# The routing weights of one tile of tokens scattered to memory instead of built by one-hot products, and the row products of the sparse tokens spread anew

## What is computed

```python
q = (xt @ w_pq).reshape(PEER_BLOCK, PEER_HEADS, 2, PEER_HALF)
s = jnp.einsum('thpd,hpkd->thpk', q, sub_keys)
v1, i1 = lax.top_k(s[:, :, 0], PEER_TOPK)
v2, i2 = lax.top_k(s[:, :, 1], PEER_TOPK)
cand = (v1[..., :, None] + v2[..., None, :]).reshape(PEER_BLOCK, PEER_HEADS, -1)
cidx = (i1[..., :, None] * N_KEYS + i2[..., None, :]).reshape(PEER_BLOCK, PEER_HEADS, -1)
top, pos = lax.top_k(cand, PEER_TOPK)
eidx = jnp.take_along_axis(cidx, pos, axis=-1)
g = jax.nn.softmax(top.astype(jnp.float32), axis=-1).astype(xt.dtype)
ue = u_tab[eidx]
a = jax.nn.gelu(jnp.einsum('thkd,td->thk', ue, xt))
ve = v_tab[eidx]
return jnp.einsum('thk,thkd->td', g * a, ve)
```

## Time and profile before

| | |
|---|---|
| median of 3 runs | 3568.3 us (3566.43 to 3577.35) |
| profiled execution: its time, its span | 3572.08 us, 3570.3 us |
| mean granted TensorE clock | 0.986 |
| PE busy | 3475.4 us, 97% of the span |
| DVE busy | 2467.0 us, 69% |
| ACT busy | 1462.7 us, 41% |
| mean rate of the DMA engines | 255 GB/s |

### The profile page before, as it was taken

One profiled execution on the slowest core, in us unless ns is written; L12 is line 12 of the kernel. 1 busy time (PEld: TensorE's weight loads), 2 busy tenths in 40 slices (PEclk: granted clock), 3 DMA queues, 4 the chain that ended last, 5 costly groups with the idle time before them and its releaser, 6 DMA issues.

```text
span 3570.3 us, 54219 instructions
## 1 busy us (share of the span) xinstructions
PE 3475.4 (97%) x18428; PEld 2973.7 (83%) x18428; DVE 2467.0 (69%) x4643; ACT 1462.7 (41%) x2544; POOL 895.4 (25%) x1026
## 2 busy tenths in 40 slices
PE   6999999999999999999999999999999999999998
PEld 5776889999999787777777777999999998777776
DVE  6455678889888775555464556888898878555554
ACT  3324233335877333333233333333367753333332
POOL 0010100003333534444400010000053345344442
PEclk9999999999999999999999999999999999999999
DMA  6354434447999998999744433444499999799995
GB/s 244 126 185 135 142 132 147 149 149 282 354 338 346 391 343 336 363 358 359 292 151 155 161 130 123 149 154 147 147 349 345 344 361 388 278 366 356 364 356 199
DMA packets 269536, 909.83 MB, mean 255 GB/s; under 512 B 32213, under 2 KB 65029, under 8 KB 268453
## 3 DMA queue, kind: packets, MB, share of 16 engines
q0 software_dynamic: 126352, 471.34, 35.9%
q1 hardware_dynamic: 106128, 385.92, 30.8%
q10 hardware_dynamic: 36868, 50.35, 3.8%
HBM read 792.14 MB, written 115.34 MB: 254 GB/s over the span
## 4 chain that ended last, share of the span: by engine, by line
PE 92%; DMA 3%; DVE 2%; issue 1%; POOL 1%; ACT 1%; SPq 0%; DVEq 0%; ACTq 0%; POOLq 0%
PE ps L441 15%; PE ps L443 15%; PE ps L442 15%; PE ps L1001 10%; PE ps L1003 9%; PE ps L1002 9%; PE ps L981 5%; PE ps L1015 3%; PE ps L810 2%; DMA urow<-in_u_rows,idu 1%; PE ps L866 1%; PE ps L937 1%; PE ps L485 1%; DMA hin<-expert_spill 1%; PE ps L887 1%
## 5 line engine op out<-in xcount | busy, mean ns | idle before, releaser
L441 PE MATMUL ps<-mov,whl 128*128 128x384 f32 (+1 forms) x2816 | 1008.8, 358 | 2.2 <-DVE whl L428 2.2
L443 PE MATMUL ps<-mov,whl 128*128 128x384 f32 (+1 forms) x2816 | 985.5, 350 | 0.0
L442 PE MATMUL ps<-mov,whl 128*128 128x384 f32 (+1 forms) x2816 | 984.2, 350 | 0.0
L428 DVE TENSOR_TENSOR whl<-raw,whl 128x1024 fp32r<-128x1024 f32 x648 | 792.5, 1223 | 206.8 <-ACT whl L418 202.5
L418 ACT CAST whl<-raw 128x1024 fp32r<-128x1024 f32 x648 | 679.5, 1049 | 87.4 <-ACT hst L1196 78.8
L1001 PE MATMUL ps<-whl,wgthl 128*128 128x512 f32 x1536 | 608.4, 396 | 19.6 <-DVE wgthl L1710 19.6
L700 POOL DMA_INDIRECT urow<-in_u_rows,idu x256 | 310.8, 1214 | 1208.8 <-DVE idu L1643 778.1
L1003 PE MATMUL ps<-whl,wgthl 128*128 128x512 f32 x1536 | 604.6, 394 | 0.0
L1002 PE MATMUL ps<-whl,wgthl 128*128 128x512 f32 x1536 | 603.4, 393 | 0.0
L441 PEld LDWEIGHTS ps<-mov,whl 128*128 128x128 f32 x2816 | 529.3, 188 | 40.1 <-issue 8.7
L442 PEld LDWEIGHTS ps<-mov,whl 128*128 128x128 f32 x2816 | 529.5, 188 | 30.5 <-issue 2.4
(11 more groups left out here) (261 smaller groups left out, 3623.0 us busy)
## 6 DMA issues: line engine op xcount, KB each, us to landing
raw<-in_uT_tab SPq DMA_DIRECT2D x256, 512.0 KB, 4.5
raw<-in_v_tab SPq DMA_DIRECT2D x256, 512.0 KB, 6.9
expert_spill<-hst ACTq DMA_DIRECT2D x256, 192.0 KB
hin<-expert_spill POOLq DMA_DIRECT2D x256, 192.0 KB, 7.9
gt<-weight_spill POOLq DMA_DIRECT2D x64, 768.0 KB, 8.8
weight_spill<-stage POOLq DMA_DIRECT2D x22, 2048.0 KB, 14.7
raw<-in_w_in SPq DMA_DIRECT2D x72, 512.0 KB, 4.7
raw<-in_w_mod SPq DMA_DIRECT2D x64, 512.0 KB, 3.6
```

The lines of the kernel that those rows point to most:

```text
L428: nc.vector.tensor_tensor(whl[:, m % RING, 1], raw[:, raw_n(m) % RAW], whl[:, m % RING, 0].bitcast(F32), ALU.subtract).then_inc(lo_done, 1)
L441: nc.tensor.matmul(o, w[:, 0, k], src[:, 0, k, :cols], start=(k == 0), stop=False)
L442: nc.tensor.matmul(o, w[:, 0, k], src[:, 1, k, :cols], start=False, stop=False)
L443: mm = nc.tensor.matmul(o, w[:, 1, k], src[:, 0, k, :cols], start=False, stop=(k == KC - 1))
```

## The change

The dense tokens are divided again. Two tiles (256 tokens, `OH`) keep the one-hot groups, 32 of them. The weights of the third tile (`N_TS = 1`) are no longer computed by PE: its part of `weight_spill` is filled with zeros at the start of each layer, four writes of 2 MB from a tile of zeros, and in each head the 16 weights of its 128 tokens are added there by 16 indirect DMAs of 128 single numbers each (`scatter_one`). DVE works out the places (`chosen`), and the softmax is made head by head (`shares`, with the exponential on ACT at slot 9 of each head).

The panels that stood beside the 16 groups move into the heads (`T_U = 10`, 12 panels for a head). The row products start in the second head: six beside each head but the first (42), then 12 in the first rest, 40 beside the 32 groups, 4 in the second rest, and 30 ahead of panel 23 of the second table. At the start of layer 0 the first two panels are split four and three chunks earlier.

```diff
-N_G = SD // GT
+N_TS = 1
+OHB = DB - N_TS
+OH = OHB * P
+N_OH = OH // TB
+N_G = OH // GT
-T_U = 8
+T_U = 10
-DOTS_V = 24
-DOTS = [0, 0] + [2] * (REST - 2) + [1, 2] * (N_G // 2) + [2] * (REST - 2) + [0, 0] + [1, 1, 2] * (DOTS_V // 3)
+DOTS_H = (0, 0, 0, 0, 0, 0, 0, 0, 0, 2, 2, 2)
+DOTS_A = sum(DOTS_H) * (PH - 1)
+DOTS_V = 23
+DOTS = ([0, 0] + [2] * (REST - 2) + [1, 1, 1, 2] * (N_G // 4) + [1] * 4 + [0] * (REST - 4)
+        + [1, 1, 2] * 7 + [1, 1])
...
+            for b in range(N_OH, NTB):
+                pool.dma_start(g_d[:, :, b].rearrange("a p x -> p a x"),
+                               zero[:].unsqueeze(1).to_broadcast([P, P // AG, P])).then_inc(zero_out, 16)
...
+            def scatter_one(h, n):
+
+                k, t = h * TOPK + n // N_TS, n % N_TS
+                settle(pool)
+                pool.indirect_dma_start(g_d.rearrange("a p b (x o) -> (a p b x) o", o=1),
+                                        bass.IndirectOffsetOnAxis(idg[:, t, k:k + 1], 0),
+                                        topv[:, OHB + t].rearrange("p h k -> p (h k)")[:, k:k + 1], None,
+                                        compute_op=ALU.add).then_inc(sc_out, 16)
+
+            def scatter(h):
+
+                pool.wait_ge(idg_ready, l * PH + h + 1)
+                pool.wait_ge(g_norm, l * PH + h + 1)
+                pool.wait_ge(sc_out, l * (16 * N_TS * SLOTS) + 16 * N_TS * TOPK * h)
+                for n in range(N_TS * TOPK if h + 1 < PH else 0):
+                    scatter_one(h, n)
...
+            for h in range(PH):
+                pool.wait_ge(idu_ready, l * PH + h + 1)
+                if h == 0:
+                    for k in range(UR):
+                        gather_u(k)
+                scatter(h)
+                if h + 1 < PH:
+                    for k in range(h * sum(DOTS_H), (h + 1) * sum(DOTS_H)):
+                        gather_u(k + UR)
...
                     if k + UR < SLOTS:
                         gather_u(k + UR)
+                    if left:
+                        scatter_one(PH - 1, left.pop(0))
...
                 if r == 1:
...
+                    pool.wait_ge(sc_out, (l + 1) * (16 * N_TS * SLOTS))
                     load_g(0)
                     load_g(1)
...
-                if not (l or which) and c >= KC - 3 and c < KC - 1:
-                    split_hi(act, l, c - (KC - 3))
+                if not (l or which) and c in (1, 3):
+                    split_hi(act, l, c // 2)
...
+                    if j == 9:
+                        act.wait_ge(g_sub, l * PH + h + 1)
+                        nc.scalar.activation(topv[:, :, h], topv[:, :, h], ACT.Exp).then_inc(g_exp, 1)
...
-                if not (l or which) and c >= KC - 1:
-                    split_lo(dve, l, c - (KC - 1))
+                if not (l or which) and c in (3, 5):
+                    split_lo(dve, l, c // 2 - 1)
...
+            def chosen(h):
+
+                hs = slice(h * TOPK, (h + 1) * TOPK)
+                first, second = sel1[:, OHB:DB, h], sel2[:, OHB:DB, h]
+                nc.vector.scalar_tensor_tensor(idf[:, 0, hs], sel1[:, DB, h], float(NKEYS), sel2[:, DB, h], ALU.mult, ALU.add)
+                nc.vector.scalar_tensor_tensor(place[:, 1], second, float(NTB * AG), first, ALU.mult, ALU.add)
+                chain.link(nc.vector.tensor_scalar(place[:, 0], first, -1.5, 0.25, ALU.add, ALU.mult))
...
                 for j in range(2 + T_U):
                     split_lo(dve, l, M_T + h * (2 + T_U) + j + LEAD)
                     if j < 2 and h:
                         key_of(h - 1, j)
+                    if j == 1 and h:
+                        chosen(h - 1)
+                    if j == 10:
+                        shares(h)
+                    if h:
+                        at = (h - 1) * sum(DOTS_H)
+                        dots_between(at + sum(DOTS_H[:j]), at + sum(DOTS_H[:j + 1]))
```

More of the change, by code:

```diff
@@ L164, in dots_by @@
 def dots_by(p):
-    return sum(DOTS[:p + 1])
+    return DOTS_A + sum(DOTS[:p + 1])
 assert dots_by(LATE_U + DOTS_V - 1) == SLOTS
@@ L295, in build_trunk @@
     dinv = sb("dinv", [P, TT * PH])
-    sel1T = sb("sel1T", [P, S])
-    sel2T = sb("sel2T", [P, S])
-    gT = sb("gT", [P, SD])
+    sel1T = sb("sel1T", [P, OH + P])
+    sel2T = sb("sel2T", [P, OH + P])
+    gT = sb("gT", [P, OH])
+    place = sb("place", [P, 3, N_TS, TOPK])
+    idg = sb("idg", [P, N_TS, SLOTS], U32)
     idf = sb("idf", [P, 2, P])
@@ L640, in _ @@
         pool.wait_ge(consts_made, 2)
+        for q in range(P // TB):
+            nc.gpsimd.iota(tokat[q * TB:(q + 1) * TB], [[P * AG, N_TS]], base=(N_OH + q) * AG * TB, channel_multiplier=1,
+                           allow_small_or_imprecise_dtypes=True).then_inc(tokat_made, 1)
         for half in range(2):
@@ L919, in _, with turn_rows @@
             spread_root(pe, 2, l * 4 + 4, l * 2 + 2)
+            def turn_rows():
+                for c in range(KC):
+                    o = ps[:, 4 + c // 4, c % 4 * P:(c % 4 + 1) * P]
+                    nc.tensor.matmul(o, mov[:, 0, c, SD:], identr[:], start=True, stop=False)
+                    mm = nc.tensor.matmul(o, mov[:, 1, c, SD:], identr[:], start=False, stop=True)
+                mm.then_inc(htok_turned, 1)
             def two_heads(two, first=False):
@@ L952, in experts @@
                         gemm(pe, l, first_m + j, more=i * 4, more_half=i * 2, cols=SD)
-            for c in range(KC):
-                o = ps[:, 4 + c // 4, c % 4 * P:(c % 4 + 1) * P]
-                nc.tensor.matmul(o, mov[:, 0, c, SD:], identr[:], start=True, stop=False)
-                mm = nc.tensor.matmul(o, mov[:, 1, c, SD:], identr[:], start=False, stop=True)
-            mm.then_inc(htok_turned, 1)
             for n in range(REST):
@@ L971, in _ @@
             settle(pe)
-            with pe.Fori(0, NTB // 2) as b:
+            with pe.Fori(0, N_OH // 2) as b:
                 for half in range(2):
@@ L1610, in key_of, with shares @@
                 chain.link(nc.vector.tensor_reduce((sel1, sel2)[side][:, :, h], eq[:], AX, ALU.add))
+            def shares(h):
+                dve.wait_ge(g_exp, l * PH + h + 1)
+                sums, share = den[:, h * TT:(h + 1) * TT], topv[:, :, h]
+                chain.link(nc.vector.tensor_reduce(sums, share, AX, ALU.add))
+                chain.link(nc.vector.reciprocal(dinv[:, h * TT:(h + 1) * TT], sums))
+                nc.vector.tensor_tensor(share, share, dinv[:, h * TT:(h + 1) * TT].unsqueeze(2).to_broadcast([P, TT, TOPK]),
+                                        ALU.mult).then_inc(g_norm, 1)
@@ new lines, in chosen @@
+            def chosen(h):
[4 more added lines that the diff above has]
+                chain.link(nc.vector.tensor_scalar(place[:, 0], first, -1.5, 0.25, ALU.add, ALU.mult))
+                nc.vector.tensor_scalar(idu[:, hs], idf[:, 0, hs], lbase[:], None, ALU.add).then_inc(idu_ready, 1)
+                chain.link(nc.vector.tensor_scalar(place[:, 0], place[:, 0], MAGIC, MAGIC, ALU.add, ALU.subtract))
+                chain.link(nc.vector.scalar_tensor_tensor(place[:, 2], place[:, 0], float(P * NTB * AG - AG), place[:, 1],
+                                                          ALU.mult, ALU.add))
+                if l == 0 and h == 0:
+                    dve.wait_ge(tokat_made, P // TB)
+                for t in range(N_TS):
+                    last = nc.vector.tensor_scalar(idg[:, t, hs], place[:, 2, t], float(TB), tokat[:, t:t + 1],
+                                                   ALU.mult, ALU.add)
+                last.then_inc(idg_ready, 1)
@@ L1612, in _, with dots_between @@
+            def dots_between(k0, k1):
+                for k in range(k0, k1):
+                    if k == 0:
+                        dve.wait_ge(htok_ready, l + 1)
+                    dve.wait_ge(u_in[k % UR], l * 16 * len(range(k % UR, SLOTS, UR)) + 16 * (k // UR + 1))
+                    nc.vector.tensor_tensor_reduce(urow[:, k % UR], urow[:, k % UR], htok[:], 1.0, 0.0, ALU.mult, ALU.add,
+                                                   act_in[:, k:k + 1]).then_inc(dot_done, 1)
             for h in range(PH):
```

85 lines of the change are left out of this document (41 added, 44 removed).

## The result

The changed kernel takes 3530.7 us (median of 4 runs, 3527.8 to 3532.0); the kernel before took 3567.4 us beside it (4 runs). The ratio is 0.9879, 95% interval 0.9866 to 0.9892. It is faster by 1.2%, 37 us, where 80 us were forecast; 3530.7 lies above the range of 3478 to 3522. The profiled execution has a span of 3526.1 us, 44.2 less than before.

The account below looks back on a forecast made before the run. PE, busy for 97% of the span, was taken as the bound. The terms 57.2 + 1.3 + 21.0 + 3.5 - 3.0 = 80.0 us off the median 3568.3 gave 3488 us, with a range of 3478 to 3522.

Parts of the forecast that it names:

- part 8: Turn from heads to first rest: 12 gathers and 12 scatters on POOL, 26 us of 25; 1 us allowed each layer.
- part 6: Sixteen scatters a head on POOL, priced at a gather's median, 1.1 us each; 0 on the path.
- part 7: Four zero writes of 2 MB in the mixers, 14.7 us each, sharing with w_in panels; 1 us allowed.
- Part 1: Sixteen groups fewer a layer, their panels moved into heads of 54.3 us; 57.2 us gained on PE.
- Part 2: Transposes on PE, 8 instead of 11, 6 records fewer in a layer; 1.3 us gained in two layers.
- Part 3: Entry to the second table: fewer row products and gathers ahead, whole delay gone; 21.0 us gained, bounds 0 and 21.0.
- the entry stays late: Rival at the second table: weight loads still wait for blocks and scatters; 3498 us if half stays, 3509 if all; chance 0.12.
- Part 4: Start of layer 0: earlier splits let PE begin at 46.4 instead of 49.97; 3.5 us gained, bounds 0 and 3.5.
- Part 5: DVE beside the heads: its work sums to 52.0 to 52.6 us of 54.3 and just fits; taken as 0.
- The rival of DVE as the bound: In the heads, each us of DVE above 54.3 costs 14 us; 2 us too much gives 3516; chance 0.14.
- the rival of slow scatters: In the heads, scatters above 3.0 us on POOL make rows late; at 4 us about 3716; chance 0.09.
- more than I count: Waits of 1.5 and 3.4 us at panel 28 of the second table also go, 3480 us; chance 0.05.

Follow-up runs that it names:

- b_entry: Kernel before with only its row products spread anew, four instead of twelve in the second rest; 3554.4 us, ratio 0.9954 to before.
- sc_spread: Changed kernel with the last head's 16 scatters begun at the ninth group, one beside each gather; 3515.7 us, ratio 0.9846 to the kernel before.
- sc_plain: Changed kernel with scatters that write instead of adding; 3516.9 us, ratio 0.9845 to the kernel before.
- z_late: Changed kernel with the four zero writes of each layer moved behind gate writes 12, 16, 20 and 24; 3519.8 us, ratio 0.9859 to the kernel before.
- align: Changed kernel with one empty tile of 32 bytes behind the new tile tokat; 3507.9 us, ratio 0.9820 to the kernel before.
- b_wgthl: Kernel before with an empty tile of 32 bytes ahead of wgthl alone; 3586.0 us, ratio 1.0035 to before.
- combo: Changed kernel with the empty 32-byte tile behind tokat, zeros behind gate writes, and last head's scatters from the ninth group; 3483.2 us, ratio 0.9750 to before.
- combo_v: combo with the first eight gathers for the second table's quads sent one a panel from panel 23; 3484.8 us, ratio 0.9751 to the kernel before.

## Why the prediction was wrong

Three steps failed: part 8's allowance of 2 us for the turn (the price of a scatter, from part 6), part 7's of 1 us for late panels, and the second table's pace, which no part touched and the sum so left at nothing. In the order of the parts:

**Part 1, right.** Heads are 54.36 us (54.3 forecast), and once the scatters are out of the way the group stages are 187.1 us, so that 54.8 of the 57.2 us are there: 95.2 us less a group stage, 67.8 more in heads and the turn behind them.

**Part 2** was 1.3 us, and 0.6 us is seen: a transpose is one record of PE, not two, so that three records went in a layer and not six. **Part 3, right, with one cause misread.** The stall is gone (1159.00 above, 0.26 us), 18.8 of 21.0 us; the rival "the entry stays late" did not happen. b_entry gives the size without anything else, 16.4 us. The long first panel, 4.1 of the 21.0 us, was read as part of DVE's delay; it was the half clock that came with the stall. It went with the stall, and waits for the second weight took some of its place.

**Part 4, right at the start, its worth not shown.** PE's first product is 3.9 us earlier; at the end of the mixers no more is seen than executions differ by.

**Part 5, right.** In the head's window DVE is busy for 50.21 of 54.36 us, and a first search still waits for the scores, to be held against the earlier trace rows:

```profile
638.14 0.89 DVE L1605 MAX8 v<-ps 128x8 f32<-128x128 f32 x4 [1.74 <-PE ps L1001]
...
692.52 0.89 DVE L1605 MAX8 v<-ps 128x8 f32<-128x128 f32 x4 [1.74 <-PE ps L1001]
```

54.38 us apart. The rival of DVE as the bound did not happen.

**Part 6, a wrong price.** A scatter was taken as a gather's median, 1.1 us; it took 1.85 us and 0.30 between. Sixteen of them and six gathers are 37.3 us of POOL in a head, 44 with the gaps, which is still under 54.3, so in the heads the error cost nothing, and the rival of slow scatters, which needs 3.0 us, did not happen. The rule of the Trainium skill that spoke against this part ("SBUF — State Buffer", "SBUF: two separate sides") is about an operation of DVE that takes both ports, and gives some 3.1 us for a transfer beside one. This trace neither bears it out nor refutes it: no scatter took more than 2.65 us, but beside each of the long ones stands a split, a row product, a comparison or a sum, which has two inputs in SBUF and is not the copy that the rule's figure is for. The gathers of at most 1.99 us, which the prediction set against the rule, stood beside splits, row products and comparisons too and were no test of it. What the trace shows is that the 50 scatters with only DVE's searches beside them took 1.55 to 1.59 us, and all that took longer than 1.59 had an operation with two inputs beside them; the one at 937.52 above, beside a row product and the masks' comparisons, took 2.65.

**Part 8, the first step that failed.** It put 12 gathers and 12 scatters at 24 x 1.1 = 26 us of 25 and allowed 1 us in each layer. At the measured 4.23 us a pair, 12 of them take some 50, and the backlog runs on to 979 us. sc_spread and sc_plain put the cost at 5.3 us in each group stage (3.30 and 2.90 of waiting, 1.7 of half clock) and 12 us in all by the ratios, where 2 were allowed.

**Part 7, the second.** "I allow 1 us for late panels" stands where 6.9 us were lost in layer 1 alone (7 in all by the ratios, 11 by the medians). The sum of the bytes was right and beside the point: 8 MB were put where the panels come just in time. Each write took 23.5 us to land, not 14.7, and in 40 us of layer 1 ACT waited 25.8 us for panels, against 4.0 in z_late.

**What no part had: the place of `wgthl`.** The largest loss, 20.5 us by the pace and 21 us by align, came from a 32 byte tile and changed sizes ahead of `wgthl`. The prediction took the other panels of the second table as unchanged without a reason; forecast and range had no term for it. The other two misses alone, 12 and 7 us less the 3 allowed, would have ended near 3504, inside the range.

**The case "more than I count"** did happen in part: the waits at panels 28 and 29 gave 8.9 us. That was luck as far as the forecast goes, and it hid some of the loss. Part of it is no gain of the change either: b_wgthl has most of it from the slower pace alone. align, at 4.12, keeps some 6 us of it.

With the three undone, combo and combo_v are 90 us below the kernel before beside them, where 80 were forecast. Of the 88.1 us between the spans of combo_v and the kernel before, 8.6 are in the second tables behind the first panel, where nothing was forecast, so that 79.5 are left for the parts. Those that were costed from rows were right in the sum, and the misses were in what was not costed (a place) or costed by the wrong neighbour (a plain gather for an adding scatter, a write beside no loads for one beside loads).

## What to carry to other kernels

A change that adds or resizes a tile moves every tile behind it: sum the sizes, see by what the operands that PE loads move, and compare the pace of stages that the change doesn't touch. Cost a new kind of transfer on POOL by pairs with what stands between, in the stretch where POOL has least room, and put it behind what others wait for. A write that nothing waits for still belongs where the engines' share is low, not where loads land just in time. And price a wait of PE with the half clock that may come with it: here a wait of 3.30 us cost 5.

## What the hardware showed that was not expected

- PE's pace with 128x128 weights in fp32r and 512 columns depends on where the weights start: 18 matmuls in 4.08, 4.12 or 4.20 us for 0, 64, and 32 or 96 bytes behind a multiple of 128, a spread of 2.9%, at a granted clock of 1.00 and with no wait (seventeen kernels).
- An indirect scatter of 128 single numbers that adds costs POOL at least 1537 ns, the same without adding 955 ns, a gather of 128 rows of 4 KB 932 ns.
- Both reach about 1.1 us more than that at times: gathers 2002 ns, adding scatters 2647. The long ones lie beside operations of DVE with two inputs in SBUF (splits, row products, comparisons): the 50 scatters without one took 1.55 to 1.59 us, the 39 with one beside them for at least 90% of their time 1.92 in the median. No run took those operations away.
- The granted clock fell from 1.00 to 0.50 during waits of PE of 7.23 and 5.97 us and 1.1 us behind the end of one of 3.30 us, and stayed there for 6.8, 6.8 and 3.4 us. The second table's products came every 0.43 us in it instead of every 0.23. Behind the wait of 1.32 us in b_entry it stayed at 1.00.
